# Mean squares of the first attention's query and key tiles: one fp32 product, or two fp32r products of high and low parts

## The reference, cut to what matters

```python
def rms_norm(x, g):
    xf = x.astype(jnp.float32)
    y = xf * lax.rsqrt(jnp.mean(xf * xf, axis=-1, keepdims=True) + EPS)
    return (y * g.astype(jnp.float32)).astype(x.dtype)
...
q = rms_norm(q.reshape(b, s, N_Q_HEADS, HEAD_DIM), q_norm_g)
k = rms_norm(k.reshape(b, s, N_KV_HEADS, HEAD_DIM), k_norm_g)
v = v.reshape(b, s, N_KV_HEADS, HEAD_DIM)
o = sliding_window_attention(q, k, v, sinks) * jax.nn.silu(z_a)
```

## Time and profile before

| | us |
|---|---|
| median of 3 runs | 2440.23 |
| the profiled execution | 2440.13 |
| its span, first to last instruction | 2438.4 |
| TensorE busy | 2413.1 (99%) |
| VectorE busy | 1568.0 (64%) |
| GpSimd busy | 1370.0 (56%) |
| ScalarE busy | 1099.5 (45%) |

### The profile page before, as it was taken

The page is one execution under the profiler, slowest core; times in us unless marked ns, Lnnn a source line. Parts: engine busy times, 40 slices in busy tenths (PEclk is TensorE's granted clock), DMA queues, the critical chain, the costliest instruction groups (busy, mean ns, idle before and its releaser), DMA issues. The chain is left out here.

```text
span 2438.4 us, 35805 instructions
## 1 busy us (share of the span) xinstructions
PE 2413.1 (99%) x11528; PEld 1996.0 (82%) x11528; DVE 1568.0 (64%) x2281; ACT 1099.5 (45%) x2030; POOL 1370.0 (56%) x1221
## 2 busy tenths in 40 slices
PE   9999999999999999999999999999999999999999
PEld 7788888888888878888888888777888888888887
DVE  8655552344677785435666666756868777777886
ACT  6333233301666661126777777832433333344442
POOL 4788887443455554443222222254289888666683
PEclk9999999999999999999999999999999999999999
DMA  4222223589210015332111111431133333487652
GB/s 144 67 80 68 61 76 109 181 282 328 76 35 26 26 35 189 125 111 70 61 61 60 60 60 61 157 120 52 63 106 124 116 116 113 149 274 222 187 181 87
DMA packets 128949, 275.65 MB, mean 113 GB/s; under 512 B 14144, under 2 KB 14528, under 8 KB 128848
## 3 DMA queue, kind: packets, MB, share of 16 engines
q1 hardware_dynamic: 83712, 155.75, 20.3%
q10 hardware_dynamic: 45136, 118.67, 13.5%
HBM read 206.41 MB, written 67.96 MB: 113 GB/s over the span
## 5 line engine op out<-in xcount | busy, mean ns | idle before, releaser
L683 POOL TENSOR_SCALAR whi<-raw 128x512 fp32r<-128x512 f32 x190 | 136.4, 718 | 335.1 <-PE bank L903 170.5
L685 POOL TENSOR_TENSOR wlo<-raw,whi 128x512 fp32r<-128x512 f32 x190 | 266.5, 1403 | 15.9
L698 POOL TENSOR_TENSOR wlo<-a,whi 128x512 fp32r<-128x512 f32 x114 | 163.6, 1435 | 41.4 <-ACT whi L1905 41.2
L903 PE MATMUL bank<-b_lo,whi 128*128 128x512 f32 x448 | 175.3, 391 | 0.0
L903 PE MATMUL bank<-a_hi,whi 128*128 128x512 f32 x400 | 158.2, 396 | 2.4 <-DVE a_lo L2819 1.4
L966 PE MATMUL bank<-b_hi,whi 128*128 128x512 f32 x384 | 156.9, 409 | 0.2 <-ACT f_raw L1684 0.2
L966 PE MATMUL bank<-b_hi,wlo 128*128 128x512 f32 x384 | 150.7, 392 | 0.0
L966 PE MATMUL bank<-b_lo,whi 128*128 128x512 f32 x384 | 150.2, 391 | 0.0
L811 POOL COPY fc<-fc 128x128 f32<-128x128 f32 x96 | 28.0, 292 | 192.9 <-DVE mx L2749 192.9
L1905 ACT ACTIVATE whi<-a 128x512 fp32r<-128x512 f32 x114 | 70.7, 627 | 133.7 <-PE bank L1246 51.6
L903 PE MATMUL bank<-b_hi,whi 128*128 128x512 f32 x320 | 125.3, 392 | 1.0 <-ACT up_g L2305 0.6
(11 more groups left out here) (793 smaller groups left out, 7870.8 us busy)
## 6 DMA issues: line engine op xcount, KB each, us to landing
raw<-in_w SPq DMA_DIRECT2D x202, 256.0 KB, 2.6
a<-in_pairs SPq DMA_DIRECT2D x152, 256.0 KB, 2.7
fc<-c_scr ACTq DMA_DIRECT2D x32, 512.0 KB, 3.6
wd_scr<-wd SPq DMA_DIRECT2D x55, 256.0 KB, 5.4
wd<-in_down SPq DMA_DIRECT2D x44, 256.0 KB, 4.9
xs_scr<-made ACTq DMA_DIRECT2D x40, 256.0 KB, 2.6
h_scr<-up_y ACTq DMA_DIRECT2D x13, 512.0 KB, 2.6
raw<-wd_scr SPq DMA_DIRECT2D x26, 256.0 KB, 3.0
```

What stands on the lines that cost most here:

```text
L683: nc.gpsimd.tensor_scalar(hi, src, 1.0, 1.0, ALU.mult, ALU.mult).then_inc(w_hi, 1)
L685: nc.gpsimd.tensor_tensor(lo, src, hi.bitcast(F32), ALU.subtract).then_inc(w_lo, 1)
L698: nc.gpsimd.tensor_tensor(ring[1][pos], src[:].rearrange("p (k c) -> p k c", c=P), ring[0][pos].bitcast(F32), ALU.subtract).then_inc(ww_lo, 1)
L903: last = nc.tensor.matmul(psum_ap, ws[w][:, k, :], a[:, kt, hs(h)], start=(first and i == 0 and j == 0), stop=(final and i == n - 1 and j ...
```

## The change

The squares are no longer given to TensorE as one float32 operand. ScalarE writes its square as a high part in fp32r (`sq_hi`). VectorE squares the same tile again in float32 and subtracts the high part (`square_lo`, two operations for each half, each of two operands in SBUF). TensorE makes two fp32r products with `head_mean`, which is now fp32r too (one more GpSimd copy at the start). The product waits for VectorE's subtraction (semaphore `q_n`, which now counts five for each tile), no longer for ScalarE's square. `sq_hi` lies where the gate `s_z` lies, so ScalarE waits for the gated output of the pair before (`og`) ahead of the first query half and not ahead of the gate. In the pairs the first mean stands five depth steps later, behind `values(0)` and `flip_p(1)`, and ScalarE's logarithm behind the exponentials of step 2; the second mean stands one depth step later.

```diff
-            def mean_square(n, h, dst, square):
+            def mean_square(n, h, dst, square_hi, square_lo):
 
-                pe.wait_ge(sw.q_sq, n * 2 + (h + 1))
-                nc.tensor.matmul(dst, head_mean[:], square[:, hs(h)], start=True, stop=True).then_inc(sw.q_ms, 1)
+                pe.wait_ge(sw.q_n, n * 5 + (2 * h + 2))
+                nc.tensor.matmul(dst, head_mean[:], square_hi[:, hs(h)], start=True, stop=False)
+                nc.tensor.matmul(dst, head_mean[:], square_lo[:, hs(h)], start=False, stop=True).then_inc(sw.q_ms, 1)
...
                 scores(2)
                 fill(0, 1, range(2))
-                pe.wait_ge(sw.lo, st + 1)
-                mean_square(n, 0, flip[:], s_sq)
                 values(0)
                 flip_p(1)
                 fill(0, 1, range(2, 7))
+                pe.wait_ge(sw.lo, st + 1)
+                mean_square(n, 0, flip[:], sq_hi, sq_lo)
                 scores(3)
                 fill(0, 1, range(7, KT))
                 values(1)
-                fill(1, 0, range(2))
+                fill(1, 0, range(3))
                 pe.wait_ge(sw.exp, st * 4 + 12)
-                mean_square(n, 1, score[0][:, 0:HALF], s_sq)
-                fill(1, 0, range(2, 3))
+                mean_square(n, 1, score[0][:, 0:HALF], sq_hi, sq_lo)
...
+            def square_lo(n, h, t, raw, square, hi, lo):
+
+                dve.wait_ge(tile_out[h], t + 1)
+                v.tensor_tensor(square[:, hs(h)], raw[:, hs(h)], raw[:, hs(h)], ALU.mult).then_inc(sw.q_n, 1)
+                dve.wait_ge(sw.q_n, n * 5 + (2 * h + 1))
+                dve.wait_ge(sw.q_sq, n * 2 + (h + 1))
+                v.tensor_tensor(lo[:, hs(h)], square[:, hs(h)], hi[:, hs(h)].bitcast(F32), ALU.subtract).then_inc(sw.q_n, 1)
...
                 normalise(1)
                 maxima(2)
+                query_lo(0)
                 add(0)
                 low(1)
                 normalise(2)
                 maxima(3)
+                query_lo(1)
                 add(1)
                 normalise(3)
...
             for c, (gain, hi, lo) in enumerate(((C_KG, s_k[0], sk_lo[0]), (C_KG, s_k[1], sk_lo[1]), (C_QG, s_q, None))):
+                for h in range(2):
+                    square_lo(c, h, U_SWA + c, early[2 * c], early[2 * c + 1], early_hi[c], early_lo[c])
                 normed(c, gain, early[2 * c], early[2 * c + 1])
```

More of the change, by code:

```diff
@@ L252, in build @@
         mask_r = fixed("mask_r", [P, 3 * P], F32R)
-        head_mean = fixed("head_mean", [P, P], F32)
+        head_mean = fixed("head_mean", [P, P], F32R)
         feat_mean = fixed("feat_mean", [P, P], F32)
@@ L282, in build @@
         early_raw = overlay(b_lo_at + 16 * 1024, *((f"early_raw{b}", [P, HALF], F32) for b in range(2)))
-        (mask_f,) = overlay(b_hi_at, ("mask_f", [P, 3 * P], F32))
+        mask_f, head_mean_f = overlay(b_hi_at, ("mask_f", [P, 3 * P], F32), ("head_mean_f", [P, P], F32))
         def psum(name, n):
@@ L313, in build @@
         early = [s_o[:, j, :] for j in range(KT)]
+        sq_hi, sq_lo = overlay(over_at + 24 * 1024, ("sq_hi", [P, S], F32R), ("sq_lo", [P, S], F32R))
+        early_hi, early_lo = (sq_hi, sp_lo, sq_hi), [b_hi[:, 2 * c + 1, :] for c in range(3)]
         v_flips = [[score[1][:, h * HALF:(h + 1) * HALF] for h in range(2)], [flip[:], bank[1][:]]]
@@ L655, in _ @@
             nc.gpsimd.memset(mask_f[:], 0.0).then_inc(const_made, 1)
-            nc.gpsimd.memset(head_mean[:], 0.0).then_inc(const_made, 1)
+            nc.gpsimd.memset(head_mean_f[:], 0.0).then_inc(const_made, 1)
             pool.wait_ge(const_made, 6)
@@ L667, in _ @@
             for h in range(2):
-                nc.gpsimd.memset(head_mean[h * DH:(h + 1) * DH, h * DH:(h + 1) * DH], 1.0 / DH).then_inc(const_made, 1)
+                nc.gpsimd.memset(head_mean_f[h * DH:(h + 1) * DH, h * DH:(h + 1) * DH], 1.0 / DH).then_inc(const_made, 1)
             pool.wait_ge(const_made, 12)
@@ L671, in _ @@
             nc.gpsimd.tensor_scalar(mask_r[:], mask_f[:], 1.0, 1.0, ALU.mult, ALU.mult).then_inc(const_made, 1)
+            nc.gpsimd.tensor_scalar(head_mean[:], head_mean_f[:], 1.0, 1.0, ALU.mult, ALU.mult).then_inc(const_made, 1)
             settle = settler(pool)
@@ L1298, in _ @@
                     tile(j * 2 + (U_MIX + 2 + c), j * 2 + (U_MIX + 2 + c), c, b_hi, b_lo)
-            pe.wait_ge(const_made, 14)
+            pe.wait_ge(const_made, 15)
             pe.wait_ge(prepared, 6)
@@ L1308, in _ @@
                             pe.wait_ge(sw.q_std, 2 * (c - 1))
-                        mean_square(c - 1, h, score[0][:, hs(h)], early[2 * c - 1])
+                        mean_square(c - 1, h, score[0][:, hs(h)], early_hi[c - 1], early_lo[c - 1])
             for t in range(2):
@@ L1553, in v_hi, with raw_and_square @@
                                      src.rearrange("p (b h d) -> p b h d", h=2, d=DH), ACT.Copy).then_inc(at.v_hi, 1)
-            def raw_and_square(src, t, n, h, raw, square):
+            def raw_and_square(src, t, h, raw, square_hi):
                 act.wait_ge(tile_done[h], t + 1)
@@ L1559, in raw_and_square @@
                 act.wait_ge(tile_out[h], t + 1)
-                nc.scalar.activation(square[:, hs(h)], raw[:, hs(h)], ACT.Square).then_inc(sw.q_sq, 1)
+                nc.scalar.activation(square_hi[:, hs(h)], raw[:, hs(h)], ACT.Square).then_inc(sw.q_sq, 1)
             def log_mean(src, n, h, square):
@@ L1573, in normed_hi @@
             def normed_hi(dst, n, raw):
-                act.wait_ge(sw.q_n, n + 1)
+                act.wait_ge(sw.q_n, n * 5 + 5)
                 for hh, rows in enumerate(head_rows):
@@ L1620, in query @@
                 def query(h):
-                    raw_and_square(bank[0], it * 4 + u0, n, h, s_raw, s_sq)
+                    raw_and_square(bank[0], it * 4 + u0, h, s_raw, sq_hi)
                 def gate_a(h):
@@ L1652, in window_pair @@
                 act.wait_ge(sw.q_lo, it * 4 + (2 * pp + 6))
+                act.wait_ge(sw.og, it * 8 + 4 * pp)
                 query(0)
-                log_mean(flip[:], n, 0, s_sq)
                 fold(0)
@@ L1657, in window_pair @@
                 expo(2)
+                log_mean(flip[:], n, 0, s_sq)
                 query(1)
@@ L1664, in window_pair @@
                 nc.scalar.preload_act_table_set("exp_and_others")
-                act.wait_ge(sw.og, it * 8 + 4 * pp)
                 gate_a(0)
@@ L1961, in _ @@
                 nc.scalar.activation(cv_v[:, hs(h)], third_bank[h], ACT.Silu).then_inc(tile_out[h], 1)
-            act.wait_ge(const_made, 14)
+            act.wait_ge(const_made, 15)
             act.wait_ge(w_lo, 3 * 2 + 2)
@@ L2118, in early_square @@
                 for h in range(2):
-                    raw_and_square(bank[h], U_SWA + c, c, h, early[2 * c], early[2 * c + 1])
+                    raw_and_square(bank[h], U_SWA + c, h, early[2 * c], early_hi[c])
             def early_root(c):
@@ L2628, in low, with query_lo @@
                     window_low(it, pp, s)
+                def query_lo(h):
+                    square_lo(n, h, it * 4 + u0, s_raw, s_sq, sq_hi, sq_lo)
                 def add(s):
```

## The result

| | before | changed |
|---|---|---|
| median, us | 2439.19 (5 runs, 2437.32 to 2440.41) | 2467.28 (5 runs, 2464.31 to 2469.42) |
| ratio to before | | 1.0112, 95% interval 1.01 to 1.0123 |
| profiled execution, us | 2440.13 | 2467.05 |
| its span, us | 2438.4 | 2465.3 |

A forecast was written before the change was run, and what follows sets the result against it. TensorE, busy 2413.1 of 2438.4 us, was taken to bound the kernel. The terms, -8.0 + 6.0 + 8.7 + 8.5 + 4.8 + 16.1 + 0.1 = +36.2, made 2440.1 into 2476 us, range 2457 to 2484.

The forecast's parts named there:

- Term 1: TensorE's 20 mean products: two fp32r products take 0.46 in place of 0.86, 8.0 us off in all.
- Term 2: First early mean: TensorE waits 3.6 and 2.4 for VectorE, taking turns with GpSimd's splits, 6.0 us; bounds 3.2 and 7.2.
- Term 3: Early means of tiles 1 and 2: VectorE's order puts the square behind `normed_lo`, so TensorE waits 8.7 and 8.5 us.
- Term 4: TensorE's clock: half clock for 3.4 us behind each of three early waits, 3 x 1.6 = 4.8 us.
- Term 5: The seven pairs: first mean in time, TensorE waits 2.25 us at the second, 7 x 2.3 = 16.1 us; bounds 0 and 24.5.
- the 7 named: Sign at early mean 1: a wait under 7 us would show that VectorE's order doesn't bind as read.
- the 1 named: Sign in the pairs: a wait under 1 us would show that the turns are not taken as counted.
- Rival A: Pairs: second mean in time or nearly; 2460 us without any wait, 2467 with 1.0 a pair; chance 0.25.
- Costed at nothing or 0.1: Earlier wait for `og`, logarithm behind step 2's exponentials, and GpSimd's extra constant copy: together taken as 0.1 us.

The follow-up runs named there:

- x_nolow: Changed kernel without VectorE's squares and subtractions, both products taking the high part: 2431.95 us, ratio 0.9965 to before.
- x_later: Changed kernel with the second mean of a pair one depth step and a flip later: 2468.13 us.
- x_turn: Changed kernel with one more VectorE operation of 128x4 ahead of `neg_max` of step 3 in every pair: 2468.27 us, ratio 1.0116 to before.
- x_swap: Changed kernel with the low parts of early tiles 1 and 2 made right behind the `normed` of the tile before, ahead of `down_sums` and `normed_lo`: 2445.58 us.
- x_oldplace: Changed kernel with the first mean of a pair put back behind the first two depth steps: 2496.89 us, ratio 1.0234 to before.
- x_act: Changed kernel with the pairs' float32 square made by ScalarE, VectorE only subtracting: 2462.58 us.
- x_best: Changed kernel with early low parts behind the previous tile's `normed` (tile 0's ahead of `down_sums(8)`) and ScalarE making the pairs' float32 square: 2435.43 us.

## Why the prediction was right, and where 9 us too high

- **Term 1** (20 products, 8.0 us off): measured. The period without low parts falls by 0.80 for two products, and x_nolow by 8.5 us in all.
- **Terms 2 and 3** (6.0, 8.7 and 8.5, together 23.2): measured 2.9 + 7.7 + 7.4 = 18.1 of idle time, and 0.9 for the second halves of tiles 1 and 2 as 2 x 0.47, 19.0 in all. Term 2 is the mis-sized one. It took GpSimd's splits at 595.61; they came at 596.70, behind the first square, so that no split lay ahead of the first subtraction. The start of GpSimd's splits was left at its old time, though it hangs on TensorE's own course, and TensorE came 1.1 later. Its lower bound, 3.2, was the better value for this execution, but by luck: it turns on how two separate times fall, the landing of the transfer that starts VectorE's sums, and TensorE's arrival. With the same order the first wait was 1.50 in x_later, 1.51 in x_turn and 1.71 in x_swap, and 3.23 in x_oldplace, where the sums ended at 595.87 and the first split started at 595.67, nearly as the forecast had them; 3.37 in x_act. The second wait was 1.95 to 1.97 in all six. So the term measures 2.9 to 5.3, and the 6.0 was high in each. Term 3 holds as an order: mean 1 came 7.7 us behind tile 2 (7.8 forecast), mean 2 7.4 behind tile 3 (7.6 forecast).
- **Term 4** (4.8 of clock): 6.6 by the windows. Three stretches, but only the first has the length of the earlier trace rows; behind the long waits the clock was down longer. It lies inside the bounds given (0 to 9.6). Together terms 2 to 4 give 25.6 measured against 28.0.
- **Term 5** (7 x 2.3 = 16.1) is the step that failed: 6.6 measured. The first mean in time: right. `neg_max` of step 3 blocked: wrong by 0.07 us in the changed kernel, and x_turn shows that it doesn't matter. The failing step is the count behind it, "L683 to 690.65, the second square to 691.2, L685 to 692.4, the subtraction to 693.0". It gave GpSimd a turn between `neg_max` and the square, and so three splits ahead of the subtraction. In both kernels there are two, one L688 and one L686: behind a blocked `neg_max` the square starts with no split between them (706.23 and 707.10 in the changed kernel, 714.02 and 715.26 in x_turn). In the rows shown, the operation that started first went first, whichever engine's; strict turns are not the rule. This is read from start times alone, and no run tested it by itself. One L688 less is 1.2 us; 2.25 less 1.2 is 1.05, against 0.67 to 0.74 measured. Of the 0.95 a pair, 0.67 is this wait; the rest is partly the refilling behind it (the two products take 0.57 to the next instruction, 716.70 to 717.27, where 0.46 is two at 0.23), and partly open.
- **What would make it wrong.** Mean 1's wait of 7.7 is over the 7 named. The pair's wait of 0.67 is under the 1 named: the turns are not taken as counted, so by its own sign the forecast was wrong in the pairs. Rival A described this: in time or nearly, 2460 without any wait, 2467 with 1.0 a pair. The pairs went A's way and the time is A's, 2467. It lies in the range because the range was drawn wide enough to hold A, not because term 5 held. That A's figure is met to 0.3 us is partly luck too: its early waits and clock were 2.4 us too high, and 2.1 us that it doesn't have came in at the start and the end (below).
- **Costed at nothing or 0.1**: at the start of the run 1.1 us came in. At 14.83 TensorE waits 0.73 for VectorE's `a_lo`, whose eight operations take 7.02 where they took 5.98; GpSimd's split of the first `early_raw` weights starts at 11.62, when its transfer lands, in place of 12.27, and so falls beside them. The change's extra copy isn't the cause: x_later, x_oldplace and x_best have it too, their split starts at 12.20 to 12.55, and they have no such wait. In the six kernels whose split starts between 11.54 and 11.88 it is there, 0.71 to 0.73. So these 1.1 us go by when the transfer landed in an execution. Whether the change moves that landing, one trace of each kernel can't tell.
- **Sum by the trace**: -8.0 + 18.1 + 0.9 + 6.6 + 6.6 + 1.1 = +25.3, of the 26.9 of the spans. Another 1.0 came in behind the pairs, where nothing was changed: from the last `values` to the end it is 1534.4 us, before it was 1533.4, and the ten traces range from 1532.4 to 1535.0. 0.6 us are not assigned.
- **Two-operand work at a shared port.** The Trainium skill, "SBUF — State Buffer", Who interferes with whom, has the later of two such instructions blocked fully; the 1.80 of the square beside the split of 713.77 and the 1.13 of L687 beside the square agree. By the Mode Summary of "Advanced Engine Details and Errata" alone no wait in the pairs was due: two operations of 0.69 behind 713.83 would end at 715.2, and TensorE came at 716.03. The 0.67 stands against it.

## What to carry to other kernels

A cheaper operand for the engine that sets the time is worth its whole saving only if whoever makes it is early: read the queue of the maker, up to the last instruction ahead of the new one, and put the new one where its input is ready, not beside the work that belongs to the same tile. Here the same instructions in another order moved the time by 28 us, the saving being 8. Where a wait sits on a chain without slack, moving it down the chain moves it and no more; shortening the chain (another engine makes one of its steps) does help.

## What was not expected of the hardware

- VectorE and GpSimd don't alternate strictly: behind a blocked 128x4 operation (0.96 and 1.33 in place of 0.23) the next 128x512 one ran unblocked at 0.68, and GpSimd's split waited (1.13 in place of 0.62). It had started 0.03 us ahead of the split, with VectorE's blocked operation not quite over.
- Waits of TensorE of 2.8 to 3.1 us were followed by half clock in two of the seven pairs of x_oldplace and not in the others, and the idle 2.9 us near 88 us in nine of the ten traces. The clock was down for 3.4, 6.8 and about 10 us around waits of 0.99 + 1.95, 7.72 and 7.43.
